# Two seams of a fused diffusion step: the norm's scale of three chunks of tokens on GpSimd, not on VectorE

## The reference

```python
def rmsnorm(x, g):
    y = x * lax.rsqrt(jnp.mean(x * x, axis=-1, keepdims=True) + EPS)
    return y * g

# in trunk, for each layer i; f is the mixer, then the feed-forward network
u = rmsnorm(x, norm_gain[i, 0]) * (1 + sc1) + sh1
y = mixer(u)
x = x + g1 * rmsnorm(y, norm_gain[i, 1])
u = rmsnorm(x, norm_gain[i, 2]) * (1 + sc2) + sh2
f = conv_ffn(u)
x = x + g2 * rmsnorm(f, norm_gain[i, 3])
```

## Time and profile before

| | us |
|---|---|
| median of three runs | 1898.85 |
| the profiled execution | 1899.4 |
| its span in the profile | 1897.6 |
| TensorE busy | 1860.9 (98%) |
| VectorE busy | 905.0 (48%) |
| ScalarE busy | 623.0 (33%) |
| GpSimd busy | 122.1 (6%) |

### The profile page before, as it was taken

One profiled execution on the slowest core, in us unless ns is written; L12 is line 12 of the kernel. 1 busy time (PEld: TensorE's weight loads), 2 busy tenths in 40 slices (PEclk: granted clock), 3 DMA queues, 4 the chain that ended last, 5 costly groups with the idle time before them and its releaser, 6 DMA issues.

```text
span 1897.6 us, 27239 instructions
## 1 busy us (share of the span) xinstructions
PE 1860.9 (98%) x11143; PEld 1670.4 (88%) x11143; DVE 905.0 (48%) x1682; ACT 623.0 (33%) x884; POOL 122.1 (6%) x145
## 2 busy tenths in 40 slices
PE   6999999999999999999999999999999999999998
PEld 5778987699978999888999999997788998899987
DVE  4416445565633565345442343436246563365633
ACT  4333233553311333244322222223235332233312
POOL 4101110010000000021000000000000000000002
PEclk8999999999999999999999999999999999999999
DMA  9934632733354222223222321326521322322221
GB/s 273 341 138 81 76 117 78 257 88 89 111 191 98 67 66 88 67 81 121 84 78 73 106 66 50 117 89 236 187 66 45 88 66 68 89 80 75 66 89 56
DMA packets 191971, 204.09 MB, mean 108 GB/s; under 512 B 8155, under 2 KB 157395, under 8 KB 188307
## 3 DMA queue, kind: packets, MB, share of 16 engines
q1 hardware_dynamic: 179075, 179.55, 31.6%
q0 software_dynamic: 4736, 12.66, 2.8%
q10 hardware_dynamic: 8080, 10.74, 1.7%
HBM read 190.28 MB, written 8.45 MB: 105 GB/s over the span
## 4 chain that ended last, share of the span: by engine, by line
PE 88%; DVE 6%; issue 2%; ACT 2%; DMA 1%; POOL 1%; SPq 0%; DVEq 0%; POOLq 0%; ACTq 0%
PE PJ L1963 42%; PE AT L1973 12%; PE PJ L2142 9%; PE PJ L1973 8%; PE PJ L2113 2%; PE AT L2017 2%; PE AT L1942 2%; PE AT L2337 1%; PE PJ L2017 1%; PE AT L2353 1%; DVE h_both L1352 1%; DVE uT L1335 1%; PE AT L2292 1%; PE AT L2350 1%; PE AT L2178 1%
## 5 line engine op out<-in xcount | busy, mean ns | idle before, releaser
L1963 PE MATMUL PJ<-h_both,w_high 128*128 128x320 f32 x3584 | 674.6, 310 | 0.0
L1963 PEld LDWEIGHTS PJ<-h_both,w_high 128*128 128x128 f32 x3584 | 562.4, 188 | 3.0 <-issue 1.7
L1779 DVE SCALAR_TENSOR_TENSOR sq<-PJ,cols,sq 128x127 f32<-128x127 f32 (+4 forms) x504 | 188.9, 430 | 237.4 <-ACT sq L1182 216.3
L1963 PE MATMUL PJ<-h_both,w_low 128*128 128x320 f32 x1280 | 291.6, 309 | 0.0
L1368 DVE TENSOR_TENSOR w_low<-ring,w_high 128x2048 fp32r<-128x2048 f32 (+1 forms) x64 | 142.1, 2220 | 167.5 <-ACT w_high L837 167.5
L1963 PEld LDWEIGHTS PJ<-h_both,w_low 128*128 128x128 f32 x1280 | 214.1, 188 | 0.0
L837 ACT ACTIVATE w_high<-ring 128x2048 fp32r<-128x2048 f32 (+1 forms) x64 | 118.8, 1856 | 204.9 <-PE PJ L1973 140.1
L2142 PE MATMUL PJ<-w_high,h_both 128*128 128x256 f32 (+1 forms) x672 | 160.2, 329 | 0.0
L1382 DVE TENSOR_TENSOR ring_low<-ring,w_high 128x2048 fp32r<-128x2048 f32 x37 | 84.6, 2286 | 130.6 <-ACT w_high L855 129.6
L1182 ACT ACTIVATE sq<-PJ,cols 128x640 f32<-128x640 f32 x80 | 70.9, 886 | 184.0 <-PE PJ L1963 184.0
L2142 PEld LDWEIGHTS PJ<-w_high,h_both 128*128 128x128 f32 x672 | 114.4, 190 | 15.7 <-issue 4.3
(11 more groups left out here) (331 smaller groups left out, 2663.1 us busy)
## 6 DMA issues: line engine op xcount, KB each, us to landing
ring<-in_ffn_w_up SPq DMA_DIRECT2D x88, 512.0 KB, 5.1
ring<-in_ret_w_in SPq DMA_DIRECT2D x24, 1024.0 KB, 7.6
ring<-in_ffn_w_down SPq DMA_DIRECT2D x40, 512.0 KB, 4.7
hT<-in_ada_w SPq DMA_DIRECT2D x14, 1024.0 KB, 6.9
ring<-in_ml_w_in SPq DMA_DIRECT2D x12, 1024.0 KB, 12.7
xT<-in_ada_w SPq DMA_DIRECT2D x11, 1024.0 KB, 7.0
turn<-in_ada_w SPq DMA_DIRECT2D x8, 1024.0 KB, 6.1
ring<-in_ret_w_out SPq DMA_DIRECT2D x6, 1024.0 KB, 5.1
```

Of the source, the lines that this page charges most:

```text
L1779: ins = v.scalar_tensor_tensor(o, z, scalar, o, ALU.mult, ALU.add)
L1963: ins = pe.matmul(PJ[:, s, b, 0:HALF], w[:, at + k * step:at + k * step + P], x[:, k, b * HALF:(b + 1) * HALF], start=(k == 0 and n == 0), ...
```

## The change

In the first and third seam, for chunks 0, 1 and 2, VectorE takes only the reciprocal, which then counts a new semaphore, x_recip. GpSimd waits for it, multiplies the residual's rows by the reciprocal into y_tok (a tensor_scalar of 128x1024), waits for its own result (pool_own), multiplies that by the row of pre factors (a tensor_tensor of 128x1024), and counts xs_pool. TensorE's transposes of these chunks wait for xs_pool; those of chunks 3 and 4, and all of the second seam, wait for xs_ready, whose counts are adapted. [...]

```diff
--- before.py
+++ after.py
@@ -301,8 +301,9 @@
         factor_ready, row_out, row_in = sem("factor_ready"), sem("row_out"), sem("row_in")
         y_squared, y_std, t_ready, end_out = sem("y_squared"), sem("y_std"), sem("t_ready"), sem("end_out")
         x_new, x_std, xs_ready, xs_turned = sem("x_new"), sem("x_std"), sem("xs_ready"), sem("xs_turned")
+        x_recip, xs_pool = sem("x_recip"), sem("xs_pool")
         uh_tok, ul_tok = sem("uh_tok"), sem("ul_tok")
-        dve_own, act_own = sem("dve_own"), sem("act_own")
+        dve_own, act_own, pool_own = sem("dve_own"), sem("act_own"), sem("pool_own")
 
         GROUPS = [A_HEADS // 2, B_HEADS // 2]
         HK = [A_HEADS * DK, B_HEADS * DK]
@@ -344,6 +345,8 @@
         ROWS_IN = (96, 192, 288, 352)
         PART_RUNS = CH * len(LAST_UNITS[0])
         LEAD = 2 * P
+        POOL_S = 3
+        DVE_S = (CH - POOL_S, 2 * CH - POOL_S, 3 * CH - 2 * POOL_S)
 
         block = ctx.enter_context(nc.Block())
 
@@ -622,6 +625,13 @@
                     pool.dma_start(pre_rows[grp], rows_dram[gap, 1, grp:grp + 1, :].to_broadcast([P, D_MODEL])
                                    ).then_inc(row_in, 16)
 
+            def scale_rows(gap, c):
+
+                pool.wait_ge(x_recip, POOL_S * gap // 2 + c + 1)
+                pool.tensor_scalar(y_tok[:, c, :], x_tok[:, c, :], x_rstd[:, c:c + 1], None, ALU.mult).then_inc(pool_own, 1)
+                pool.wait_ge(pool_own, POOL_S * gap // 2 + c + 1)
+                pool.tensor_tensor(y_tok[:, c, :], y_tok[:, c, :], pre_rows[min(c, 1)], ALU.mult).then_inc(xs_pool, 1)
+
             def post_product(gap, nh, c):
 
                 y = y_tok[:, c, nh * WIDE:(nh + 1) * WIDE]
@@ -732,12 +742,15 @@
                                     XI[:, d, ds(g * 2 + hh, 1), :].to_broadcast([P, CH - 1, P]),
                                     ALU.mult).then_inc(qz_ready, 1)
                 if layer == 0:
+                    pool.wait_ge(row_in, ROWS_IN[0])
+                    for c in range(POOL_S):
+                        scale_rows(0, c)
                     pool.wait_ge(bank_read, READ_AT[1])
                     read_post(1)
                     pool.wait_ge(factor_ready, 4)
                     write_rows(1, 1, pre_a[:, 0, :, :])
                     pool.wait_ge(row_out, 128)
-                    pool.wait_ge(xs_ready, CH)
+                    pool.wait_ge(xs_ready, DVE_S[0])
                     read_pre(1)
                     pool.wait_ge(factor_ready, 5)
                     write_rows(2, 0, post_a[:, 0, :, :])
@@ -759,6 +772,9 @@
                     pool.wait_ge(row_out, 192)
                     read_pre(2)
                     write_rows(3, 0, post_a[:, 1, :, :])
+                    pool.wait_ge(row_in, ROWS_IN[2])
+                    for c in range(POOL_S):
+                        scale_rows(2, c)
                     pool.wait_ge(row_out, 224)
                     pool.wait_ge(bank_read, READ_AT[3])
                     read_post(3)
@@ -1340,7 +1356,11 @@
                         ins.then_inc(x_new, 1)
                 elif kind == "s":
                     v.wait_ge(x_std, CH * gap + c + 1)
-                    link(v.reciprocal(x_rstd[:, c:c + 1], x_rstd[:, c:c + 1]))
+                    ins = v.reciprocal(x_rstd[:, c:c + 1], x_rstd[:, c:c + 1])
+                    if gap % 2 == 0 and c < POOL_S:
+                        ins.then_inc(x_recip, 1)
+                        return
+                    link(ins)
                     v.scalar_tensor_tensor(y_tok[:, c, :], x_tok[:, c, :], x_rstd[:, c:c + 1], pre_rows[min(c, 1)],
                                            ALU.mult, ALU.mult).then_inc(xs_ready, 1)
                 else:
@@ -1976,7 +1996,10 @@
 
             def turn_scaled(gap, c):
 
-                pe.wait_ge(xs_ready, CH * gap + c + 1)
+                if gap % 2 == 0 and c < POOL_S:
+                    pe.wait_ge(xs_pool, POOL_S * gap // 2 + c + 1)
+                else:
+                    pe.wait_ge(xs_ready, DVE_S[gap] - CH + c + 1)
                 for h in range(2):
                     if c == 0:
                         pe.wait_ge(bank_read, READ_AT[gap] + (14 if gap == 1 else 5))
```

## The result

The change made the kernel slower. The median is 1905.31 us (1904.18 to 1906.45, 7 runs) against 1898.83 us (1898.17 to 1899.48, 7 runs) in the same rounds: a ratio of 1.0035, 95% interval 1.0025 to 1.0045, or +6.5 us. The forecast was 1899.0 us, with a range up to 1902.2 us. The profiled execution took 1906.29 us, with a span of 1904.5 us, so the span grew by 6.9 us.

A forecast was written before the change was run, and what follows sets the result against it. TensorE was taken to bound the kernel, with 88% of the page's chain against VectorE's 6%. The seams' +0.06 and +0.16 us made +0.2, so 1898.85 + 0.2 = 1899.0 us, range 1897.3 to 1902.2 us for 8 in 10.

The forecast's parts named there:

- What the change adds: Step pricing GpSimd's two 128x1024 passes for each of six chunks: scale 1.20 us, product 2.3 us, 3.66 us with waits.
- The product at 2.3 us: GpSimd's two-input product at 1024 columns, priced between 2.2 and 2.55 us from a row of 1.29 us at 512.
- the upper sum: Total for both seams if GpSimd's product takes 2.55 us: about +0.8 us.
- The ceiling of 1.65 us: Most that both seams could gain, since ScalarE's copies hold the u steps: 0.44 + 0.81 + 0.40 us.
- GpSimd delays x steps and not u steps: In the seams, GpSimd passes collide with VectorE's all-SBUF updates (x steps), not with u steps, which read PSUM.
- VectorE first at chunk 0 of the third seam: Chunk 1's updates on VectorE precede GpSimd's passes, starting at 1410.03 instead of 1411.35 us; chance 0.47.
- The pair at 3.66 us: Time a chunk needs from its reciprocal's end for both GpSimd passes and waits, where VectorE needed 1.3 us.
- the sum of +0.2 us: Net effect of both seams: +0.16 us in the first, +0.06 us in the third.
- slower by the pair's length: Rival: GpSimd's passes take longer, deciding from 3.6 us a pair; at 5.1 us, +4.2 us, 1903.1 us; chance 0.18.

The follow-up runs named there:

- e1: The changed kernel with a second operation in GpSimd's scale pass, adding a column of zeros; 1899.08 us against 1899.18 us for the kernel before.
- e6: Changed kernel, GpSimd's product moved ahead of a two-operation scale for chunks 0 to 2, ScalarE's unused squares put elsewhere; 1897.78 us against 1899.16 us before the change.
- e7: As e6, but for all five chunks of both seams; 1897.27 us against 1899.16 us for the kernel before the change.
- e9: The changed kernel with a second operation in GpSimd's scale pass, multiplying by the number 1.0; 1898.77 us against 1898.75 us for the kernel before.
- e2: The changed kernel with GpSimd's one-operation scale pass cut into two of 512 columns each; 1908.05 us in one run.
- e8: As e6, but with the changed kernel's one-operation scale pass; 1897.92 us against 1899.16 us for the kernel before the change.

## Why the prediction was wrong

The step that failed is the first price of "What the change adds": "the straight line, 0.836 ns a column, gives 769 + 512 x 0.836 = 1.20 us at 1024". The line is right, at 1.20 us in e1. But it was drawn through rows of another form, with two operations, and the pass of the change has one. I had looked at engine, opcode and type, which are the same, and not at the code of the line that those rows came from. The row itself shows it too: it reads three names (x_norm, pre_a, mod), where the pass of the change reads two (uT, end_mem). "For it: no row shows 1024 columns. Against: the scalar form's rows are steady" weighed the wrong unknown: the columns were safe, the form was not in the trace at all. So the earlier trace rows should have stood as a neighbour with bounds, as the product's price did, and not as the price.

The other steps, in order:

- The product at 2.3 us: 2.35 to 2.40 us. Right, inside its bounds. (Twice the row of 1.29 is 2.58 us, not 2.55; and by the terms in its bracket the upper sum is 0.2 + 0.8 = +1.0 us, not +0.8. Neither moves the range.)
- The ceiling of 1.65 us because ScalarE's copies are right behind: e6 and e7 gained 1.3 and 2.75 us over the two seams. The bound was for three chunks; three chunks stayed under it.
- GpSimd delays x steps and not u steps: right in every trace.
- VectorE first at chunk 0 of the third seam: right in e1 (1.42 us), wrong in the changed kernel and e9, where GpSimd came between the two updates. It cost the 0.85 us that the stretch shows, less than the 1.3 us won, so x1 ended 0.48 us earlier than before.
- The pair at 3.66 us and the sum of +0.2 us: with the form that I had priced, e1 measures +0.1 us over the two seams, and 0.0 (-0.9 to +1.0 permille) in the time. The mechanism was right for a kernel that was not the one asked about, and the match to 0.1 us is in part luck: in e1's third seam x3 ends 0.15 us earlier than before, where +0.06 had been forecast, and a low clock behind it, which the forecast did not have, takes 0.13 back.
- The rival "slower by the pair's length" is what happened. It gave 3.6 us as the point from which it decides and +4.2 us for a pair of 5.1 us, in three places: chunk 2 of both seams and chunk 0's transposes in the third. The pair was 5.3 us; x3's delays were +1.68 and +3.23 = 4.9 us. The longer pair is worth about +0.6 (0.2 us in three places, an estimate) over the 4.2, so the sum is close, but the path was not quite that: the rival left out that chunk 1's product stretches x2 (+0.92 us) and that 0.71 us come back before u1. The remaining 1.85 us were in none of the rivals: that TensorE, idle until GpSimd is done, falls to the 1.2 GHz level and runs its next 5.7 us slowly.

The Trainium skill's page "SBUF — State Buffer", section "Who interferes with whom", calls the ports that VectorE and GpSimd share an exclusive lock, and says, at VectorE's two-port modes, that whoever issues first has them for the whole instruction. For the product the runs agree that VectorE waits for its end: the first seam's x3 was stretched by 2.00 us with 2.20 us of the product to go, the third seam's x2 by 0.91 us with 1.12 to go. For the scale pass with one operation they do not: in the changed kernel's third seam the pass of 2.84 us came between the two updates of x1 and stretched them by 0.85 us, as much as e9's pass of 1.13 us did (2.29 - 1.42 = 0.87); in e2, where the pass comes in halves of 1.55 us, x1 took 1.85 us and was stretched by 0.43.

## What to carry to other kernels

A price from a row holds for that row's form: compare the number of operations and operands in the code of its line, not only opcode, shape and type, and where the form is missing from the trace, price it by bounds and ask at which price the plan turns. When a helper engine takes over a step, count how long its result keeps TensorE waiting, and add what the granted clock takes behind a standstill. Give a slower engine the part whose inputs are ready early, so that it runs under another engine's wait: that, and not the form, is what took the seams below those of the kernel before (e6 and e8).

## What was not expected of the hardware

- On GpSimd a tensor_scalar with one operation is slower than the same with two: 1.55 against 0.77 us at 128x512, 2.84 against 1.13 (a number) or 1.20 us (a column) at 128x1024. The page "GPSIMD Engine Reference" of the Trainium skill, section "3.1 Elementwise — side-by-side cycle accounting", tells of 769 ns for 512 elements in the best case; the form with two operations agrees, the form with one takes twice that.
- A standstill of TensorE of 4.90 us was followed by 5.7 us at a granted clock of 0.50, and cost 1.75 us in the seam beside the wait itself. A shorter one was followed by a low clock too, and cost little: in e1 TensorE waited 1.98 us before the transposes at 1426.46, the window behind has a granted clock of 0.72 (columns as above), and from the end of x3 to the last u step the seam took 14.04 us instead of 13.91.

```profile
1426.00:1432.00 6.00, 5.54 (x34) 5.54 (x35) 3.78 (x6) 4.29 (x14) 1.33 (x3) 0.72 0.01 3
```
